# The last feed-forward of the second token group: gate and up products from seven block products instead of eight, with weight sums made by accumulating transfers

## The reference

```
x <- LN1(alpha*x + 0.5*SwiGLU_1(x))
x <- LN2(alpha*x + W_mix_out[conv_group(x) | dsa_group(x)])
x <- LN3(alpha*x + MemCrossAttn(x, mem))
x <- LN4(alpha*x + 0.5*SwiGLU_2(x))

def _swiglu(x, w_gate, w_up, w_down):
    return (jax.nn.silu(x @ w_gate) * (x @ w_up)) @ w_down
```

## Time and profile before

| | |
|---|---|
| median of 3 runs | 2527.73 us (2526.59 to 2529.33) |
| span of the profiled execution | 2523.5 us |
| TensorE busy | 97% |
| DVE, ACT, POOL busy | 36%, 39%, 55% |
| moved by DMA | 245.00 MB, mean 97 GB/s |
| weight loads, queue of SP | 197.88 MB, 27.4% of 16 engines |
| granted TensorE clock, mean | 0.993 |

### The profile page before, as it was taken

How to read it: one execution, slowest core, us unless ns; L and a number is a source line. 1 busy time by engine, 2 the same in 40 slices (tenths; PEclk the granted TensorE clock), 3 DMA queues, 4 the chain that set the end, 5 groups by cost and what they waited for, 6 DMA issues and landing times.

```text
span 2523.5 us, 39960 instructions
## 1 busy us (share of the span) xinstructions
PE 2437.7 (97%) x16311; PEld 2217.3 (88%) x16311; DVE 920.9 (36%) x1775; ACT 982.3 (39%) x1736; POOL 1376.1 (55%) x860
## 2 busy tenths in 40 slices
PE   8999999999999999998999999999899999999998
PEld 8888889888999999987789877888659899999998
DVE  1000002266810004277452689997264333000003
ACT  4333333534333233455543533333473435333231
POOL 4776665534666666422252676766405246666663
PEclk9999999999999999999999999999999999999999
DMA  4444532453233222533121234333402122433322
GB/s 145 123 119 117 159 94 75 139 156 104 83 94 91 86 84 79 141 107 125 45 76 35 70 102 106 110 92 100 166 1 88 48 68 81 121 109 101 92 84 69
DMA packets 425661, 245.00 MB, mean 97 GB/s; under 512 B 23008, under 2 KB 415328, under 8 KB 424720
## 3 DMA queue, kind: packets, MB, share of 16 engines
q1 hardware_dynamic: 389712, 197.88, 27.4%
q10 hardware_dynamic: 33200, 32.56, 4.0%
q0 software_dynamic: 2576, 12.07, 1.3%
HBM read 218.79 MB, written 21.74 MB: 95 GB/s over the span
## 4 chain that ended last, share of the span: by engine, by line
PE 85%; ACT 4%; DVE 4%; POOL 3%; issue 2%; DMA 1%; ACTq 0%; DVEq 0%; POOLq 0%
PE LIN L768 77%; PE TR L1109 1%; POOL WL L2093 1%; PE LIN L845 1%; PE TR L821 1%; ACT WH L1159 1%; POOL XL L2133 1%; ACT PR L1608 1%; ACT PT L1633 1%; PE LIN L1057 1%; PE TR L922 1%; DVE SC L1714 1%; PE TR L1096 1%; DVE PR L2032 1%; DVE CB L1958 1%
## 5 line engine op out<-in xcount | busy, mean ns | idle before, releaser
L2093 POOL TENSOR_TENSOR WL<-WRAW,WH 128x1024 fp32r<-128x1024 f32 (+1 forms) x378 | 889.3, 2355 | 473.9 <-ACT WH L1159 467.5
L768 PE MATMUL LIN<-XH,WH 128*128 128x256 f32 (+3 forms) x3032 | 838.2, 317 | 20.7 <-DVE Y L1782 6.5
L768 PE MATMUL LIN<-XH,WL 128*128 128x256 f32 (+3 forms) x3032 | 830.9, 315 | 0.0
L768 PE MATMUL LIN<-XL,WH 128*128 128x256 f32 (+3 forms) x3032 | 829.3, 314 | 0.0
L768 PEld LDWEIGHTS LIN<-XH,WH 128*128 128x128 f32 (+1 forms) x3032 | 529.0, 188 | 61.0 <-issue 20.0
L768 PEld LDWEIGHTS LIN<-XL,WH 128*128 128x128 f32 (+1 forms) x3032 | 528.8, 188 | 34.0
L768 PEld LDWEIGHTS LIN<-XH,WL 128*128 128x128 f32 (+1 forms) x3032 | 526.6, 188 | 33.8
L768 PE MATMUL LIN<-HH,WH 128*128 128x256 f32 (+2 forms) x1632 | 464.6, 307 | 1.7 <-POOL HL L2174 1.7
L768 PE MATMUL LIN<-HL,WH 128*128 128x256 f32 (+2 forms) x1632 | 462.1, 305 | 0.0
L768 PE MATMUL LIN<-HH,WL 128*128 128x256 f32 (+2 forms) x1632 | 461.4, 305 | 0.0
L1163 ACT ACTIVATE FG<-LIN 128x512 f32<-128x512 f32 (+3 forms) x270 | 154.9, 575 | 740.0 <-PE LIN L768 731.9
(11 more groups left out here) (200 smaller groups left out, 2048.2 us busy)
## 6 DMA issues: line engine op xcount, KB each, us to landing
WRAW<-in_ffn_gate SPq DMA_DIRECT2D x88, 512.0 KB, 3.8
WRAW<-in_ffn_up SPq DMA_DIRECT2D x88, 512.0 KB, 3.8
WRAW<-in_ffn_down SPq DMA_DIRECT2D x64, 512.0 KB, 3.8
WRAW<-in_w_mix_in SPq DMA_DIRECT2D x44, 512.0 KB, 3.8
WRAW<-in_ffn_down SPq DMA_DIRECT2D x32, 384.0 KB, 3.3
WRAW<-in_w_mix_out SPq DMA_DIRECT2D x16, 512.0 KB, 3.9
WRAW<-in_w_mem_q SPq DMA_DIRECT2D x16, 512.0 KB, 3.9
WRAW<-in_w_mem_o SPq DMA_DIRECT2D x16, 512.0 KB, 3.8
```

The source lines that it names most:

```text
L768: last = pe.matmul(LIN[0:pr.rows, pr.slot, out:out + w], wt[:, pr.tile % RING, c, 0:pr.rows], x[:, c, col:col + w], start=(c == 0 and wt i ...
L2093: pool.tensor_tensor(WL[:, n % RING, 0:nk, 0:width], WRAW[:, n % 2, 0:nk, 0:width], WH[:, n % RING, 0:nk, 0:width].bitcast(F32), ALU.subtr ...
```

## The change

The gate matrix of the second feed-forward, cut into two halves of its rows and two halves of its columns (quarters a upper left, b lower left, c upper right, d lower right) and with the 544 tokens cut into two of 272, gives four quarter results from seven products of blocks instead of eight. Hidden tile u and tile u + 11 form a unit; units 0 and 10 stay as they were, units 1 to 9 are made by seven, gate first and then up. Only group 1 in the second feed-forward does this. A block product has 4 chunks, so 12 matmuls of 272 columns, and a weight of 4 chunks (256 KB).

- Four of the seven weights are sums of quarters of the matrix (named "ac", "cd", "acd" and "abcd" after their quarters). They are made in DRAM ahead of time: 64 transfers of 128 rows x 1408 columns (0.72 MB) issued by GpSimd, one at the end of each of the first 64 products of group 0's back, half of them plain copies and half accumulating; each waits for the one before it on the same rows, issued four products earlier.
- The tokens get four sums T0 to T3 with hi and lo parts ("token sum" and "token low" on DVE, "token high" on ScalarE), at the end of the fifth to eighth product of that feed-forward.
- The weight rings are counted in half tiles (8 places), `WRAW` in half tiles (4 places, 6 for the seven), and the lo part of a weight of the seven is made by DVE.
- The quarters are put together from four PSUM banks: ScalarE copies SA (block 0) and the left first quarter (block 4); DVE makes SU (after block 1), SV and the right second quarter (after block 3), the right first (after 5) and the left second (after 6). Block 3 waits for SU, 5 for SV, 6 for the right second quarter. Gate goes through Silu in place. At the end of an up matrix GpSimd multiplies both sides, ScalarE makes both HH, GpSimd both HL.
- The parts of the feed-forward are now [0], [1, 2], [3, 4], [5, 6], [7, 8, 9, 10] in units. The down products of part 0 are added by DVE straight from PSUM, with ALPHA in the same instruction, so the norm before no longer scales `Y` in group 1.
- The early strands go to the down products 1 and 7 of part 1, 5 of part 2 and 3 of part 3.

```diff
+SEVEN = [("raw", 0, 0), ("sum", "acd", 0), ("sum", "cd", 0), ("sum", "ac", 0), ("raw", 4, 0), ("raw", 4, 1),
+         ("sum", "abcd", 0)]
+SUM_STEPS = [("ac", "a", False), ("cd", "c", False), ("ac", "c", True), ("cd", "d", True),
+             ("acd", "ac", False), ("acd", "d", True), ("abcd", "acd", False), ("abcd", "b", True)]
...
+    def settle(self):
+        for w in self.weights:
+            over = [m for m in self.weights[:w.n] if m.start < w.start + w.blocks - 2 * RING]
+            if over:
+                over[-1].frees.append(w.n)
...
+    def ffn_by_seven(self, which, g, after_norm, norm):
+        made = []
+        for part, units in enumerate(UNIT_PARTS):
+            final = part == len(UNIT_PARTS) - 1
+            order = (1, 0) if norm is None else (0, 1)
+            for q, u in enumerate(units):
+                if u in WHOLE_UNITS:
...
+                else:
+                    for kind in ("gate", "up"):
+                        made += self.seven(which, g, kind, u, q, part)
+            tiles = [((("down", which, tuple(units)), P * d, P, 0), d, dict(kind="down", part=part)) for d in range(KD)]
+            made += self.stage("ffn", g, tiles, 2 * len(units), lambda k: final, (), order, which=which,
+                               norm=norm if final else None, rescales=part == 0)
...
+def token_strands(ffn):
+    ffn[RING].end.extend([("token sum", 0), ("token sum", 1)])
+    ffn[RING + 1].end.extend([("token sum", 2), ("token sum", 3), ("token high", 0), ("token high", 1)])
+    ffn[RING + 2].end.extend([("token high", 2), ("token high", 3), ("token low", 0), ("token low", 1)])
+    ffn[RING + 3].end.extend([("token low", 2), ("token low", 3)])
...
+            for k, pr in enumerate((mixout + memq + memo + ffn)[:2 * SUM_COUNT]):
+                pr.end.append(("weight sums", k))
...
+                downs[KD + 1 + 6 * t].end.append(("early", t))
...
@@ TensorE @@
+            def one_of_seven(pr):
+                i, m = pr.j, pr.matrix
+                before = PLAN.products[pr.p - 1]
+                await_low(pe, PLAN.weights[pr.tile])
+                if i == 0 and before.name != "seven":
+                    for k in (before, PLAN.products[pr.p - 2]):
+                        pe.wait_ge(product_read[k.slot], k.turn + 1)
+                    pe.wait_ge(tok_lo, 4)
...
+                if i == 3:
+                    pe.wait_ge(seven_mixed, 5 * m + 1)
+                if i == 4:
+                    pe.wait_ge(seven_copied, 2 * m + 1)
+                if i == 5:
+                    pe.wait_ge(seven_mixed, 5 * m + 2)
+                if i == 6:
+                    pe.wait_ge(seven_mixed, 5 * m + 3)
...
+                for c in range(4):
+                    for wt, x in ((WH, 0), (WH, 1), (WL, 0)):
+                        last = pe.matmul(seven_bank(m, i), ring_place(wt, w)[:, c, :], moving(x, c),
...
@@ ScalarE @@
+                if pr.j == 6 and pr.kind == "up":
+                    for k, side in enumerate((1, 0)):
+                        act.wait_ge(multiplied, pr.event + k + 1)
+                        act.activation(HH[:, pr.f + side, :], GU[:, 2 + side, :], ACT.Copy).then_inc(hidden_hi, 1)
...
@@ DVE @@
+                if pr.j == 1:
+                    dve.wait_ge(product, pr.p + 1)
+                    dve.wait_ge(seven_copied, 2 * m + 1)
...
+                    dve.scalar_tensor_tensor(SU[:, :], seven_bank(m, 1), -half, SA[:, :], ALU.mult, ALU.add)\
+                        .then_inc(seven_mixed, 1)
...
+                elif pr.rescales:
+                    y = Y[:, pr.j, cols(pr)]
+                    dve.wait_ge(product, pr.p + 1)
+                    dve.scalar_tensor_tensor(y, y, ALPHA, in_psum(pr), ALU.mult, ALU.add).then_inc(product_read[pr.slot], 1)
...
@@ GpSimd @@
+            def weight_sums(k):
+                matrix, k = divmod(k, SUM_COUNT)
+                step, r = divmod(k, 4)
...
+                if made:
+                    pool.wait_ge(sums_made[r], 16 * made)
...
+                if adds:
+                    pool.dma_start(dst, src, accum_op=ALU.add).then_inc(sums_made[r], 16)
+                else:
+                    pool.dma_start(dst, src).then_inc(sums_made[r], 16)
...
+            def consume_seven(pr):
+                if pr.kind != "up" or pr.j != 6:
+                    return
+                m = pr.matrix
+                for k, side in enumerate((1, 0)):
+                    pool.wait_ge(seven_mixed, 5 * m + 4 + k)
...
+                    pool.tensor_tensor(u, GU[:, side, :], u, ALU.mult).then_inc(multiplied, 1)
+                for k, side in enumerate((1, 0)):
+                    u = GU[:, 2 + side, :]
+                    pool.wait_ge(hidden_hi, pr.event + k + 1)
+                    pool.tensor_tensor(HL[:, pr.f + side, :], u, HH[:, pr.f + side, :].bitcast(F32), ALU.subtract)\
+                        .then_inc(hidden_lo, 1)
```

More of the change, by code:

```diff
@@ L154, in __init__, with tell, pieces @@
         self.event = 0
+        self.add = self.adds_before = 0
         self.tell()
-    def tell(self, which=0, after_norm=None, norm=None, kind="", f=0, part=0):
+    def tell(self, which=0, after_norm=None, norm=None, kind="", f=0, part=0, rescales=False):
         self.which, self.after_norm, self.norm = which, after_norm, norm
         self.kind, self.f, self.part = kind, f, part
+        self.rescales = rescales
+class Weights:
+    def __init__(self, n, name, c0, width, row, nk, low):
+        self.n, self.name, self.c0, self.width, self.row, self.nk, self.low = n, name, c0, width, row, nk, low
+        self.blocks = 2 if nk > 4 else 1
+        self.start = self.low_no = self.raw = self.landed = 0
+        self.frees = []
+        self.displaced = []
+    def pieces(self):
+        if self.name[0] == "down":
+            return [(2 * q, 2, u) for q, u in enumerate(self.name[2])]
+        return [(0, self.nk, None)]
 class Plan:
@@ L190, in stage @@
                     pr.tell(**facts, **more)
+                    if pr.kind == "down" and half is None and not pr.rescales:
+                        self.adds += 1
+                        pr.add = self.adds
                     made.append(pr)
@@ L223, in ffn, with hidden_of @@
             made += ups + downs
+        return made
+    def hidden_of(self, ups):
+        for pr in ups:
+            if pr.kind == "up":
+                self.events += 1
+                pr.event = self.events
+                self.hidden_done[pr.which, pr.g.index, pr.part, pr.f, pr.half] = self.events
+                for half in (0, 1) if pr.half is None else ():
+                    self.hidden_done[pr.which, pr.g.index, pr.part, pr.f, half] = self.events
+                if pr.half is not None:
+                    self.hidden_done[pr.which, pr.g.index, pr.part, pr.f, None] = self.events
@@ new lines, in seven @@
+    def seven(self, which, g, kind, u, q, part):
+        made = []
+        events = self.events
+        for i, (source, row, side) in enumerate(SEVEN):
+            if source == "sum":
+                w = self.weigh(("sum", which, kind, row), P * u, P, 0, 4, "dve", 6)
+            else:
+                w = self.weigh(f"ffn{which}_{kind}", P * (u + PAIRS * side), P, row, 4, "dve", 6)
+            pr = self.add(w.n, "seven", i, g, None, 4)
+            pr.tell(which=which, kind=kind, f=2 * q, part=part)
+            pr.matrix = self.sevens
+            pr.event = events
+            made.append(pr)
+        self.sevens += 1
+        if kind == "up":
+            self.events += 2
+            for half in (None, 0, 1):
+                self.hidden_done[which, g.index, part, 2 * q + 1, half] = events + 1
+                self.hidden_done[which, g.index, part, 2 * q, half] = events + 2
+        return made
@@ L340, in back @@
         else:
+            token_strands(ffn)
             ffn[2 * RING].mid.append(("gains",))
+            downs = [pr for pr in ffn if pr.kind == "down" and pr.half is None]
             for t in range(4):
-                ffn[12 + 12 * t].end.append(("early", t))
+                downs[KD + 1 + 6 * t].end.append(("early", t))
             last = [pr for pr in ffn if pr.half == 0][-4:]
@@ L388 @@
 TOK_AT = {0: 0, 1: len(GROUPS[0].tiles)}
-ADDED_AT = {(1, 0): 0, (1, 1): 2 * KD, (2, 0): 4 * KD, (2, 1): 7 * KD}
+ADDED_BEFORE_LAST = max(pr.add for pr in PLAN.products if pr.which == 2 and not pr.g.sample)
 EARLY = len(GROUPS[0].tiles)
@@ L539, in encoder_step @@
         spill_cl = [nc.dram_tensor(f"spill_cl{i}", [P, KC, GC], F32, kind="Internal").ap() for i in range(2)]
+        sums = {(which, kind, name): nc.dram_tensor(f"sum{which}_{kind}_{name}", [D // 2, F // 2], F32, kind="Internal").ap()
+                for which in (2,) for kind in ("gate", "up") for name in SUMS}
         def sem(name):
@@ L2139, in take_up @@
                     norm_step(*what)
+                elif kind == "weight sums":
+                    weight_sums(*what)
                 elif kind == "early":
@@ L2176, in consume_ffn @@
```

(7 more changed lines are left out.)

351 lines of the change are left out of this document (285 added, 66 removed).

## The result

The changed kernel takes 2613.55 us (median, 2604.53 to 2615.91) against 2528.53 us for the kernel before on the same chip: ratio 1.0333, interval 1.0315 to 1.0352. It is 85 us slower, where 56 was forecast.

The account below looks back on a forecast made before the run. TensorE, busy 2437.7 of 2523.5 us, bounds the kernel. Span 2523.5 - 27.1 (matmuls) + 35.0 (feed-forward stalls) + 44 (sums) + 5 (issues) = 2580, plus 4.2 to the median: 2584 us; range 2528 to 2650.

Parts of the forecast that it names:

- 27.1 saved: Gate and up of nine units: 18 matrices each drop one block product of 1.51 us, 27.1 us less.
- (a) turns: Turn from an up matrix to the next gate, five times: block 3 waits for SU, 2.5 us each, 12.6 together.
- (b) part ends: Up to down, three times: the first down product waits for GpSimd's low part, products and HLs, 4.3 us each, 12.9.
- (c) part 0: Part 0's end: ScalarE evacuates product 409 late, chunk 1 is ready 5.4 us after it; 4.7 us lost.
- (d): Blocks after a down product wait for its evacuation (four times 0.65 to 0.75), the last unit's end 0.5: 3.2 us.
- (e) early norms: One early norm on part 1's last down product puts 5.5 us ahead of DVE's low part and SU: 2.1 us.
- 16 slower: Upper bound for the last feed-forward's net change, forecast 7.9 us slower, between 3 faster and 16 slower.
- The sums, 44 and 5: First group, mixout onward: 64 transfers at 3.6 us each cost 44 us; GpSimd's issuing in two norms costs 5.
- rival 2: Sums are fast, but weights land late beside them, 3.3 us too late in seven groups: 23 more, 2564 us; chance 0.12.
- 1 (sums all but free, 2541): Sums run at the lower end, 1.8 us a transfer: 2541 us, or 2555 if adds take two reads; chance 0.20.
- 3 (an add costs over its third stream): Adding costs more than the third DRAM end, 7.2 us a transfer: sums cost 135 us, total 2676; chance 0.10.
- Rivals 4 and 5: 4: handovers as quick as bare chain, sums hidden, 2522, chance 0.10; 5: sums free, stalls about 27 us, 2528, chance 0.08.

Follow-up runs that it names:

- the frame: Changed kernel with all units made whole and no weight or token sums, keeping its parts, half-tile rings, DVE rescale and early norms: 2544.66 us (ratio 1.0060).
- all three repairs: Changed kernel with weight-sum transfers at every third product, HH copies after the next gate's block 1, early norms behind gate block 3: 2561.27 us (ratio 1.0134).

## Why the prediction was right, and where it was off

The direction and the range were right; the time was 30 us low, and that it was not further off is in part luck, since the sums came out 9 us under their price by this profile while the feed-forward came out 27 over. Of these 27 us 8 are waits (43.8 measured, 35.5 summed), 14 the clock, 1.5 the pace, and 3 are open. By its steps:

- **27.1 saved.** It holds: 192 block matmuls in a row take 24.38 us on the chain, 0.127 each, 1.5 us more over 1512 than with 0.126.
- **(a) turns, 2.5 each.** Measured 2.44 to 2.50. The chain has ScalarE's hi copy, SA, the next hi copy, DVE's low part and SU in the order worked out:

```profile
2219.32 0.62 ACT WH L1395
2219.93 0.28 ACT SA L1716
2220.22 0.53 ACT WH L1395
...
2220.83 1.50 issue
2222.33 0.44 DVE SU L2312
```

The 1.50 is DVE's low part, which ends at 2222.4, after GpSimd's second HL. With ScalarE's order changed, all five waits went.
- **(b) part ends, 4.3 each.** Measured 0.69 + 3.41, 0.69 + 3.50, 0.69 + 3.39, so 4.1. The low part of a down weight (1.26), two GU (2.65) and two HL (2.59) stand one after another on GpSimd, as said.
- **(c) part 0, 4.7.** Measured 6.88. The term named ScalarE's queue; the one that ended last was GpSimd's:

```profile
2169.79 7.34 POOL WL L2466 x6
2177.13 1.81 POOL FP L2588
...
2179.47 0.81 POOL HL L2592
```

Six small low parts of the coming down weights are ahead of the last product's FP in GpSimd's list. With them on DVE the wait fell only to 5.0, with 1.3 before it. There GpSimd sat idle for 8.3 us before FP, and the chain runs through ScalarE's token highs, the very queue of the prediction, which had lain under GpSimd's:

```profile
2148.28 1.00 ACT T3H L1801
2149.28 0.30 ACT FG L1399
...
2149.72 1.65 POOL FP L2592
```
- **(d), 0.65 to 0.75 and 0.5.** It came out at 0.7 to 0.9 each, four waits.
- **(e) early norms, 2.1.** Measured 9: 1.83, 4.46, 2.23 (of which 0.7 belong to (d)) and 1.25. The prediction followed DVE alone. The chain goes on through ScalarE's queue:

```profile
2278.31 1.30 DVE YOUT L2053
...
2279.62 0.35 ACTq L1430
...
2280.01 0.53 ACTq L1543
...
2280.94 0.63 ACT WH L1395
...
2282.20 0.45 DVE SU L2312
```

ScalarE stores the early rows, waits for DVE's last pass to do it, and the evacuations and hi copies queued behind that store are late. One norm was counted, and four land on something. Taken away, most of it returned, at the part ends above all.
- **The clock.** The sum has no term for it, so it was put at nothing. This is the step that failed most: behind waits of 2.2 to 6.9 us stand half-clock stretches, eight in this feed-forward, about 14 us. The upper bound for this feed-forward (16 slower) did not hold either: 35.
- **The sums, 44 and 5.** Measured 40 by the profile, or 49 by taking them away: the size was right and the composition was not, so the size is luck. Mixout got 14.5 longer (23 forecast), memq with memo 16.9 (21), the rest 8 (0). One price of 3.6 us for both kinds was to be the DMA engines' time per transfer. The plain copies cost 7 us, the adds 32 and the issues 10, twice their price of 5. The DMA share was 0.7 to 0.8, not near 1. GpSimd's waits for its own sums came to 10.7 us, 8.3 of them in memq, where the chain of waits stays on TensorE; what TensorE waited for were single weights that landed 10 to 12 us later than the median before, with 20 us at half clock around two of them. That weights land late was rival 2; it came true inside the forecast case. Its rule from the Trainium skill, "DMA: Bandwidth & Descriptors", Queues, rings and completion order (engines take turns between queues packet by packet), agrees in direction with 13.5 to 15.7 us beside the sums and 3.3 to 4.1 with the sums spread.
- The Trainium skill, "DMA: Bandwidth & Descriptors", Latency and other measured facts, gives 207 to 214 GB/s for copies between HBM tensors. No run here has the copies alone, so none shows that figure. Under load a plain copy of 0.72 MB landed in 5.3 to 6.3 us, and its packets took 2.0 us of the 16 engines by the estimate above, less than the 3.4 us worked out from that page of the Trainium skill. With 3.4 in place of 3.6 the prediction's own sum falls by 6 us, not by the 4 it names. Adding is not in that figure, and costs more.
- **Rivals.** 1 (sums all but free, 2541) falls with the 49 us that they cost. 3 (an add costs over its third stream) was right in that adding is the dear part: an adding transfer lands 2.6 to 4.3 us later than a copy of the same bytes at its place. But the sums together came to 49 us, not its 135 (which by its own terms should be 139, memq being 103 against 87). Rivals 4 and 5 are excluded by the kernel without sums, 35 us slower.

What stays open: 2 to 3 of the frame's 15 us, and whether its 20 us more at half clock than before, most of them outside the last feed-forward, cost anything; how the 32 us of the adds divide in the medians; and why the time at half clock differs between profiles in stages that are the same (30.7 to 44.4 us from the norm before it on, in five profiles of the same feed-forward, which is then 34.8 to 39.6 us longer than before).

## What to carry to other kernels

A block product saved is worth its columns only if the work that it moves onto other engines is off their queues when TensorE comes: here 27 us of matmuls were paid for with 44 us of waits of 0.7 to 6.9 us and 14 us of half clock that the waits brought. Price a transfer by its kind, the adding one apart from the copying one, and spread background transfers over all the stages there are (35 us here). Follow an engine's list past the instruction that was added, over each wait for another engine, since what is queued behind it is what comes late.

## What the runs showed of the hardware

**A DVE instruction on two columns took 4.8 us.** The timeline around the chain's MSQ (L2111), in which all operands are in SBUF:

```profile
1300.96 3.00 POOL L2529 TENSOR_TENSOR XL<-Y,XH 128x256 fp32r<-128x256 f32 x4
...
1302.40 4.77 DVE L2111 TENSOR_TENSOR MSQ<-MSQ 128x2 f32<-128x2 f32 x1
...
1303.70 1.04 POOL L2488 DMA_DIRECT2D sum_gate_cd<-in_ffn_gate  x1
...
1304.27 2.87 POOL L2466 TENSOR_TENSOR WL<-WRAW,WH 128x1024 fp32r<-128x1024 f32 x1
```

It starts inside one of GpSimd's four XL and ends only as GpSimd's WL ends, three instructions later, with a transfer's issue between them. Before it took 0.16 to 0.78 us. In this norm it takes 4.2 with plain copies, 3.8 with transfers of 16 columns and 0.6 without the transfers. So it hangs on the issues standing there and not on the bytes; how an issue brings it about is not shown. The Trainium skill, "SBUF — State Buffer", SBUF: two separate sides, says that of a DVE instruction with two inputs in SBUF and a GpSimd instruction that reads SBUF the one that starts first holds a shared pair of ports to its end. The 0.6 without transfers agrees, as it ended with one XL; here DVE was held through several GpSimd instructions in a row, which the rule for one instruction does not give.

**The clock can fall after short waits.** Of the eleven waits of over 2.2 us in this feed-forward the five over 3 us each left a stretch with the granted clock at 0.50 (1.2 GHz), of 6.8 us behind 6.88 and of 3.4 behind the others; of the six of 2.2 to 2.5 us three did. In the kernel without sums, which has the same waits there, four of the six did, and 10.2 us stand around 6.86. In the kernel with all three repairs 4.45 to 6.90 left 6.8, but with the early norms alone moved 5.52 left 3.4. So neither whether a wait of 2.2 to 2.5 us brings the half clock nor how long it lasts follows from the wait's length alone. With matmuls in place of most of the wait the clock stayed at 1.00 from 2130 to 2400 us.

**Adding transfers.** From DRAM to DRAM, 0.72 MB beside others: 8.1 to 10.5 us from issue to landing (medians of four), the same without adding 5.2 to 6.6. The issue takes GpSimd 0.8 to 1.0 us, a plain one 0.5 to 0.6.
